# Projection 2's first weights in quarters between output projection 1's loads, and an opening that loads the norm's row first

## The reference, cut to what matters

```
def first_block(x, ...):                    # block 1
    h = rms_norm(x, norm_gain)              # the opening: norm and projection 1
    proj = h @ w_in                         # [1024, 3328]
    ...                                     # two attentions, each gated
    mixed = concatenate([o_a, o_b])         # [1024, 1024], gated by silu(g)
    x = x + mixed @ w_out                   # output projection 1
    return rms_norm(x, final_norm_gain)

def hybrid_layer(x, ...):                   # block 2
    h = rms_norm(x, norm_w)
    proj = h @ w_in_2                       # projection 2, [1024, 4104]
    ...                                     # delta-rule branch, dilated attention branch
    return x + mixed @ w_out_2
```

## Time and profile before

| | |
|---|---|
| Runs | 1531.7 us median of 3 (1531.52 to 1535.36) |
| The profiled execution | 1534.37 us, of it 1532.6 us span from the first to the last instruction |
| PE busy | 1470.8 us, 96% of the span |
| DVE, ACT, POOL busy | 800.2, 626.7, 411.6 us |
| DMA | 103.55 MB, mean 68 GB/s over the span |
| Mean granted TensorE clock | 0.989 |

### The profile page before, as it was taken

How to read it: one execution, slowest core, us unless ns; L and a number is a source line. 1 busy time by engine, 2 the same in 40 slices (tenths; PEclk the granted TensorE clock), 3 DMA queues, 4 the chain that set the end, 5 groups by cost and what they waited for, 6 DMA issues and landing times.

```text
span 1532.6 us, 31219 instructions
## 1 busy us (share of the span) xinstructions
PE 1470.8 (96%) x12826; PEld 1287.1 (84%) x12826; DVE 800.2 (52%) x1493; ACT 626.7 (41%) x1297; POOL 411.6 (27%) x509
## 2 busy tenths in 40 slices
PE   6999999989999999998999999999998998999998
PEld 5999998868888777776799999888897887788887
DVE  5248311158888767644330616433433776888531
ACT  5322121047777567643232211343324553777310
POOL 0112132100000166632212211222114775344420
PEclk9999999999999999999999999999997999999999
DMA  7413322000000113147321435533111111212332
GB/s 241 65 49 102 98 77 90 1 1 1 1 1 1 51 62 76 52 142 168 124 56 28 60 76 90 81 57 55 28 43 56 30 38 57 98 59 75 107 124 83
DMA packets 84468, 103.55 MB, mean 68 GB/s; under 512 B 25375, under 2 KB 68543, under 8 KB 84328
## 3 DMA queue, kind: packets, MB, share of 16 engines
q1 hardware_dynamic: 84328, 101.56, 25.8%
HBM read 78.40 MB, written 23.12 MB: 66 GB/s over the span
## 4 chain that ended last, share of the span: by engine, by line
PE 51%; DVE 4%; ACT 2%; issue 1%; DMA 1%; POOL 0%; SPq 0%; DVEq 0%; ACTq 0%
PE s_ps L362 23%; PE s_ps L1291 10%; PE s_ps L2746 2%; PE s_ps L2732 2%; PE s_ps L2721 1%; PE s_ps L2162 1%; DMA qT<-s_gate 1%; PE s_ps L1117 1%; PE s_ps L1098 1%; PE s_ps L2105 1%; PE s_ps L2709 1%; PE s_ps L2120 1%; PE s_ps L2722 1%; PE s_ps L1277 1%; PE s_ps L1670 1%
## 5 line engine op out<-in xcount | busy, mean ns | idle before, releaser
L328 POOL TENSOR_TENSOR p_w_lo<-p_w_raw,p_w_hi 128x2048 fp32r<-128x2048 f32 (+1 forms) x27 | 125.4, 4646 | 526.2 <-ACT p_w_hi L312 526.2
L362 PE MATMUL s_ps<-p_w_hi,w_out_hi 128*128 128x256 f32 (+1 forms) x640 | 181.9, 284 | 0.1
L362 PE MATMUL s_ps<-p_w_hi,w_out_lo 128*128 128x256 f32 (+1 forms) x640 | 179.7, 281 | 0.0
L362 PE MATMUL s_ps<-p_w_lo,w_out_hi 128*128 128x256 f32 (+1 forms) x640 | 179.5, 281 | 0.0
L362 PE MATMUL f_ps<-p_w_hi,hT_hi 128*128 128x256 f32 x576 | 164.0, 285 | 3.0 <-DVE p_w_lo L322 3.0
L362 PE MATMUL f_ps<-p_w_lo,hT_hi 128*128 128x256 f32 x576 | 162.9, 283 | 0.0
L362 PE MATMUL f_ps<-p_w_hi,hT_lo 128*128 128x256 f32 x576 | 162.8, 283 | 0.0
L362 PEld LDWEIGHTS s_ps<-p_w_hi,w_out_hi 128*128 128x128 f32 x640 | 120.6, 188 | 0.9 <-issue 0.6
L362 PEld LDWEIGHTS s_ps<-p_w_lo,w_out_hi 128*128 128x128 f32 x640 | 120.8, 189 | 0.0
L362 PEld LDWEIGHTS s_ps<-p_w_hi,w_out_lo 128*128 128x128 f32 x640 | 120.6, 188 | 0.0
L362 PEld LDWEIGHTS f_ps<-p_w_hi,hT_hi 128*128 128x128 f32 x576 | 109.3, 190 | 3.3 <-issue 3.3
(11 more groups left out here) (296 smaller groups left out, 3627.5 us busy)
## 6 DMA issues: line engine op xcount, KB each, us to landing
p_w_raw<-w_in SPq DMA_DIRECT2D x27, 1024.0 KB, 8.4
s_gate<-p_spill SPq DMA_DIRECT2D x48, 128.0 KB, 1.8
kbT<-x SPq DMA_DIRECT2D x8, 512.0 KB, 7.0
b_w_raw<-w_out SPq DMA_DIRECT2D x8, 512.0 KB, 4.3
qT<-s_gate SPq DMA_DIRECT2D x8, 512.0 KB, 5.7
qT<-x SPq DMA_DIRECT2D x8, 512.0 KB, 3.7
s_x<-qT SPq DMA_DIRECT2D x8, 512.0 KB, 3.2
c_table<-s_line SPq DMA_DIRECT2D x8, 512.0 KB, 3.7
```

The source lines that it names most:

```text
L328: ops.tensor_tensor(self.w_lo[:, c % 2, :, 0:w], self.raw[:, :, 0:w], self.w_hi[:, c % 2, :, 0:w].bitcast(F32), ALU.subtract).then_inc(sel ...
L362: last = self.nc.tensor.matmul(out, lhs, rhs, start=(kt == 0 and i == 0), stop=(kt == KT - 1 and i == 2))
```

## The change

SP's list in output projection 1 gets a quarter of the first weight chunk (256 rows, 256 KB) after each of `load_x(2)` to `load_x(5)`, in place of the whole after `load_x(3)`. The first three quarters count on a semaphore of their own, the last on `w_loaded`. The second chunk's load moves from behind `load_x(6)` to behind `load_x(7)`, and the third's from ahead of the last two stores to behind them. ACT makes chunk 0's high part after tile 5's norms (with a wait for the first three quarters), and chunk 1's not after tile 6's norms but after the first root of tile 7, between the turned tiles 1 and 2 of projection 2. POOL makes chunk 0's low part after `mix(7)`.

In the opening, SP issues the gain row right behind x's tile 0, then the identity, then the first half of the weights, and only then the ones. ACT and DVE make the parts of the weights' first half ahead of those of the turned tile.

```
+    def load_quarter(self, sp, q):
+        ch, kt = self.chunks[0], KT // 4
+        src = self.w_dram[q * kt * P:(q + 1) * kt * P, ch.col0:ch.col0 + ch.total].rearrange("(k p) n -> p k n", p=P)
+        sp.dma_start(self.raw[:, q * kt:(q + 1) * kt, 0:ch.total], src).then_inc(self.w_loaded if q == 3 else self.quarters_loaded, 16)
...
     def first_scalar(self, act):
         self.norm.take_root_table(act)
         self.norm.std(act, 0)
+        self.split_half_hi(act, 0)
         self.norm.split_hi(act, 0)
-        self.split_half_hi(act, 0)
...
     def first_vector(self, dve):
         self.norm.prepare(dve)
         self.norm.normalise(dve, 0)
+        self.split_half_lo(dve, 0)
         self.norm.split_lo(dve, 0)
-        self.split_half_lo(dve, 0)
...
         norm.load(sp, 0)
+        norm.load_gain(sp)
         sp.dma_start(g.ident[:, :], g.ident_d).then_inc(g.ident_loaded, 16)
+        pr.load_half(sp, 0)
         sp.dma_start(g.ones[:, :], g.second["c_ones"]).then_inc(g.ident_loaded, 16)
-        norm.load_gain(sp)
-        pr.load_half(sp, 0)
...
             store(t - 2)
             load_x(t)
-            if t == 3:
-                pr.load(sp, 0)
+            if t <= 5:
+                pr.load_quarter(sp, t - 2)
             if t == 6:
-                pr.load(sp, 1)
                 line.load(sp)
...
-        pr.load(sp, 2)
+        pr.load(sp, 1)
         store(NT - 2)
         store(NT - 1)
+        pr.load(sp, 2)
...
         for t in range(NT):
             mix(t)
-            if t == 6:
-                pr.gpsimd(pool, 0, 1)
-        pr.gpsimd(pool, 1, 6)
+        pr.gpsimd(pool, 0, 6)
...
-            if t == 3:
+            if t == 5:
+                act.wait_ge(pr.quarters_loaded, 48)
                 pr.split_hi(act, 0)
-            if t == 6:
-                pr.split_hi(act, 1)
         act.wait_ge(op.job_done, 2 * NT)
         turner.split_hi(act, 0)
         square(NT - 1, 0)
         turner.split_hi(act, 1)
         root(NT - 1, 0)
+        pr.split_hi(act, 1)
```

More of the change, by code:

```diff
@@ L240, in __init__ @@
         self.half_loaded = k.sem(tag + "w_half_loaded") if self.halves == 2 else None
+        self.quarters_loaded = k.sem(tag + "w_quarters_loaded") if self.halves == 1 else None
         self.w_hi_ready = k.sem(tag + "w_hi_ready")
```

## The result

| | before | after |
|---|---|---|
| Median of the runs, us | 1532.05 (4 runs, 1531.52 to 1535.36) | 1521.28 (4 runs, 1519.0 to 1525.87) |
| Span of the profiled execution, us | 1532.6 | 1524.1 |

The ratio is 0.9935 with a 95% interval of 0.9912 to 0.9958: 10.8 us by the medians, 6.4 to 13.5 by the interval. Forecast were 9.9 us and 1521.8.

What follows compares the result with a forecast made beforehand. PE bounds the kernel (busy 1470.8 of 1532.6 us), so only its waits pay, chiefly gate 5's behind the weights. Gains of 8.3 (quarters) and 1.6 (opening) sum to 9.9: 1531.7 to 1521.8 us, range 1519.5 to 1526.5.

Steps and rivals of the forecast that it cites:

- Rival 4: Output projection 1: gate 5 was slow by itself, so the stall stays and only the opening gains; 1530.1 us, chance 0.05.
- The quarters: Output projection 1: each quarter puts 3.35 us before its gate, no gate is late, tile 4's step becomes 12.06; -8.3 us.
- margins of 4.7 to 5.1: Output projection 1: us by which the mixes of gates 4 to 7 would be ready before PE wants them.
- Rival 3: Quarters' fixed parts add up: three more DMAs at 2.6 us, all uncovered, take 7.8; 1529.6 us, chance 0.06.
- the 6.0 us: Extra fixed cost of four DMAs for one, about 2.0 us each; if all on the path, 3.9 of the gain left; none counted.
- Rival 5: Each quarter pays the slow spell anew; stalls begin at 8 us a quarter, 10.3 gives over 1536.3 us; chance 0.04.
- The cast ahead of turned tile 2: Projection 2, ACT: moved cast delays that split by up to 1.90 us, covered to within 0.1; counted 0, 1.9 if uncovered.
- POOL's low part of chunk 1: Projection 2: takes 4.62 us, there at 786.1 on the old scale; first matmul stands well behind on PE; no loss counted.
- The opening: First projection: weights' half issued one place earlier and split first, so PE starts at 13.6 instead of 15.16; -1.6 us.
- bound of 2.7: Opening: largest gain allowed, if the weights' half lands at 8.7 us; the smallest was 0.6.
- L: Opening: landing time of the weights' first half, forecast 9.8 us; PE starts at L + 3.8, so 13.6.
- rival 1: Opening: the ones, moved behind 512 KB, hold PE; landing 2 us after the half, no opening gain; 1523.4 us, chance 0.15.

Runs made afterwards that it cites:

- experiment 2: Kernel before with only the quarters and the moved loads and casts, opening as before: 1524.07 us against 1530.82, ratio 0.9957.
- experiment 5: Kernel after with the first weight chunk whole, one 1 MB load behind gate 5 and ahead of store 2: 1523.17 us against 1532.54 before, ratio 0.9959.
- experiment 11: Kernel before with chunk 0 read from the same weight tensor, rows 13 312 bytes apart instead of 16 416: 1520.81 us against 1531.4, one run each.
- experiment 12: Kernel before with chunk 0 read from the first block's weights, rows 13 312 bytes apart: 1521.27 us against 1531.4, one run each.
- experiment 7: Kernel after with three more 256 KB loads, never used, so 1 MB ahead of each of gates 4 to 7: 1530.05 us, one run, against 1532.54 before.
- experiment 3: Kernel before with the first chunk in four quarters issued back to back at the old place: 1528.61 us against 1530.82, ratio 0.999.
- experiment 4: Kernel after with POOL's low part of chunk 1 held until DVE has scaled tile 7: 1519.45 us against 1530.82 before, ratio 0.9931.
- experiment 8: Kernel after with POOL's chunk 1 low part held until tile 7's scale, ones waited for only at first use: 1520.32 us against 1532.54 before, ratio 0.9933.

## Why the prediction was right

**What bounds.** Right. Gate 5, late behind the weights, was the loss in tile 4's step, and its whole 8.3 us came back (8.3 in experiment 2). Rival 4, that the stall isn't the weights', is out by experiments 5, 11 and 12: gate 5 takes 4.7 with the weights behind it, and about 8 behind 1 MB of other rows. The 8.3 were not standing still alone: the late mix also met a DVE scale and took 2.24 in its first half, and the granted clock behind it was 0.83.

**The quarters.** Right in mechanism, the price over-sized. Forecast were 3.35 us ahead of the gate; measured are 704.8 - 697.21 - 0.44 - 4.6 = 2.5. Gates 4 to 7 land 6.8 to 7.1 after their issue and not 7.5 to 8.5, and margins of 4.7 to 5.1 became 5.5 to 5.8. The reason given for 3.35, that the poor rate goes by bytes, is wrong (experiment 7), and that the whole takes 13.4 has to do with the distance of its rows (11, 12); a quarter of the price was a fair guess all the same. Rival 3, fixed parts that add up: the margins covered them, and in experiment 3 the gate landed 1.4 us earlier behind four DMAs than behind one, counted from the first issue of the weights. So the 6.0 us that the prediction worked out for them as an estimate from the Trainium skill ("DMA: Bandwidth & Descriptors", section "Anatomy of one DMA") do not show here. Rival 5, each quarter paying anew, did not occur: at 2.5 us a quarter is far from the 8 at which stalls begin.

**The cast ahead of turned tile 2.** Right: counted 0. PE turns tile 3 without a wait in after, and in experiment 4, where the cast still stands ahead of that split, turned tile 4 waits for nothing.

**POOL's low part of chunk 1.** Missed. The prediction had it ready in time because its first matmul stands far behind on PE, and looked only at who waits for its result. What it missed is what runs beside it: from 770.24 to 774.83 DVE's scale of tile 7 was held, and 1.5 us of the lead went. Experiment 4 takes that away and gets 1.4 back. The sign was already in the trace of before: DVE's scale at 694.45 took 2.18 beside the mix of the earlier trace rows, and the next mix's first half took 2.24 at 718.77 beside a scale that had begun first. DVE's and POOL's timelines of before:

```profile
694.45 2.18 DVE L1806 SCALAR_TENSOR_TENSOR qT<-qT,att_stat,vT 128x1024 f32<-128x1024 f32 x1
...
718.58 1.28 DVE L1806 SCALAR_TENSOR_TENSOR qT<-qT,att_stat,vT 128x1024 f32<-128x1024 f32 x1
```

```profile
718.77 2.24 POOL L1647 TENSOR_TENSOR qT<-tok,qT 128x512 f32<-128x512 f32 x1 [23.21 <-DMA qT<-s_gate]
```

**The opening.** Right in kind. Between the two profiled executions it gave 2.94 instead of 1.6, just past the bound of 2.7. Two terms differ. L, the half's landing, is 7.60 and not 9.8. The chain behind it is L + 4.6 instead of L + 3.8, because the ones came 1.26 behind the half and not 0.1 to 0.5: rival 1's mechanism, at a price of 0.8. L came out early because the 7.6 us from issue to landing of the earlier trace rows, which the prediction carried over, is the longest of the seven traces with the old opening (5.9 to 7.6), and the 5.5 of after is the shortest of the six with the new one (5.5 to 6.4). By the averages of those traces the opening gained 1.8, so the forecast of 1.6 was near, and most of the 1.3 between 1.6 and 2.94 is the choice of the two executions. In experiment 8, where PE doesn't wait for the ones, the half is the next limit.

**The sum.** By these two traces, 2.9 + 8.3 - 1.5 = 9.7 against 9.9: two differences, +1.3 in the opening and -1.5 at the seam, nearly cancel, which is luck. With the opening at its average, 1.8 + 8.3 - 1.5 = 8.6. The medians say 10.8 with 6.4 to 13.5 and can't tell these sums apart. Part of the spread lies in the stretches at half clock, whose lengths differ between executions: 25 runs of the unchanged kernel in the first group of experiments reach from 1526.74 to 1537.79. That the median came within 0.6 us of the forecast says nothing of the two small terms.

## What to carry to other kernels

When one queue carries both the operands of a running loop and the weights of the next stage, put the weights behind the operand with the nearest due time; whether they are cut matters less than that. An operation that is moved to another time on an idle engine has to be checked against what runs beside it: a long POOL instruction on SBUF that meets a DVE instruction with two SBUF operands can hold it until it has ended, even if nobody waits for POOL's result. When a transfer's rate is poor, read as many bytes from rows at another distance before blaming its size. And a term of 1 to 3 us that is read from one trace should be read from several executions of the same code first: here the old opening alone moved by 2 us.

## What the runs showed of the hardware

**POOL and DVE exclude one another in some operations.** DVE's scale with two SBUF operands took 3.85 beside a POOL subtraction of 4.59 and ended 1.09 after it; moved apart, 1.28 (experiment 4). In output projection 1 of before, DVE's scale lost twice (2.18 and 1.62) and POOL's mix once, 2.24 in place of 1.31, beside a scale of 1.28 that had started 0.19 earlier. In after, DVE's second scales of four tiles took 1.66 to 1.91 there and the first halves of two mixes 1.90 and 1.98; no step grew by it. The one that started second ended 1.07 to 1.09 us after the first when it was DVE, and 1.15 to 1.17 when it was POOL. DVE's low parts, with one operand in PSUM, ran beside POOL at their usual time. The Trainium skill ("SBUF — State Buffer", section "Who interferes with whom") has this as a rule: a DVE instruction with two SBUF inputs contends with a GpSimd instruction that reads SBUF, and issue order decides which of the two is blocked. The traces agree with it, with the numbers above.

**1 KB pieces moved at under half the rate.** Rows 16 416 bytes apart: 127 to 134 GB/s at a DMA share near 1. Rows 13 312 bytes apart: 290 GB/s with the gate's traffic in the same window. In the records of the packets, 1 KB took 46 to 48 ns on average in experiment 11 and 127 to 259 in before. The other loads of before go the same way: nine chunks of 1 MB of the first block's weights, 13 312 apart, landed 5.2 to 6.4 us after their issue, and the ten of about 1 MB of the second block's, 16 416 apart, after 8.2 to 17.4. So the distance is not the whole of it: chunk 0 was the slowest of those ten, and the second took 10.3. In experiment 7 neighbouring columns of the same rows, read right after, were quick, while the touch 60 us ahead did not help. The two distances differ in alignment too (13 312 is a multiple of 1024, 16 416 only of 32), and no run separates distance from alignment. What happens in the memory stays open. The Trainium skill ("DMA: Bandwidth & Descriptors", section "Latency and other measured facts") has lower rates at row distances that are large powers of two, down to 103 GB/s at 4 MiB, where 192 bytes more did not restore the rate. No run here has such a distance.
